# Layer norm of a streaming encoder layer: normalising on ScalarE, weight and bias as two plain VectorE operations

## What is computed

```python
def layer_norm(x, g, b):
    mu = xf.mean(-1); var = square(xf - mu).mean(-1)
    return ((xf - mu) * rsqrt(var + LN_EPS)) * g + b

def layer(x, ...):
    x = layer_norm(ALPHA * x + 0.5 * swiglu(x, ffn1_w_up, ffn1_w_down), ln1_g, ln1_b)
    h, new_buf, S_new = mixer(x, ...)      # one wide projection, short convolution, 4 retention heads, w_out
    x = layer_norm(ALPHA * x + h, ln2_g, ln2_b)
    x = layer_norm(ALPHA * x + 0.5 * swiglu(x, ffn2_w_up, ffn2_w_down), ln3_g, ln3_b)
```

## Time and profile before

| | before |
|---|---|
| median of 3 runs | 1916.72 us |
| lowest to highest | 1916.34 to 1918.64 us |
| the profiled execution | 1916.19 us, of which 1914.4 us are the span from first to last instruction |
| TensorE busy / VectorE busy / ScalarE busy / GpSimd busy | 1847.2 / 1109.4 / 463.7 / 650.9 us |
| mean granted TensorE clock | 0.987 of full |

### The profile page before, as it was taken

One profiled execution on the slowest core, in us unless ns is written; L12 is line 12 of the kernel. 1 busy time (PEld: TensorE's weight loads), 2 busy tenths in 40 slices (PEclk: granted clock), 3 DMA queues, 4 the chain that ended last, 5 costly groups with the idle time before them and its releaser, 6 DMA issues. The chain is left out here.

```text
span 1914.4 us, 26761 instructions
## 1 busy us (share of the span) xinstructions
PE 1847.2 (96%) x11200; PEld 1718.6 (90%) x11200; DVE 1109.4 (58%) x1395; ACT 463.7 (24%) x771; POOL 650.9 (34%) x428
## 2 busy tenths in 40 slices
PE   7899999998999999999999999999998899999996
PEld 6889899896889989989989999999987799899895
DVE  7667585577455355354354455334438677585666
ACT  4224243241061051051051000000004234242240
POOL 4323232232423423423423443444433233243230
PEclk9999999998999999999999999999998999999998
DMA  7333324403746646636647544444454323324312
GB/s 288 122 108 103 122 78 132 132 23 117 264 137 235 223 133 241 218 132 246 214 132 250 180 151 143 148 154 154 151 172 163 122 89 121 122 72 138 121 46 99
DMA packets 90328, 286.80 MB, mean 150 GB/s; under 512 B 8928, under 2 KB 11360, under 8 KB 89952
## 3 DMA queue, kind: packets, MB, share of 16 engines
q1 hardware_dynamic: 36288, 132.14, 22.4%
q0 software_dynamic: 24768, 90.19, 13.2%
q10 hardware_dynamic: 29152, 62.76, 8.9%
HBM read 260.86 MB, written 24.19 MB: 149 GB/s over the span
## 5 line engine op out<-in xcount | busy, mean ns | idle before, releaser
L391 POOL TENSOR_TENSOR wl<-raw,wh 128x1024 fp32r<-128x1024 f32 x172 | 434.1, 2524 | 92.5 <-DMA wh<-in_weights 89.8
L454 PE MATMUL ps<-xh,wl 128*128 128x320 f32 x1280 | 400.7, 313 | 22.6 <-POOL wl L391 14.0
L454 PE MATMUL ps<-xl,wh 128*128 128x320 f32 x1280 | 399.2, 312 | 0.0
L454 PE MATMUL ps<-xh,wh 128*128 128x320 f32 x1280 | 399.0, 312 | 0.0
L382 POOL DMA_DIRECT2D wh<-in_weights x172 | 97.2, 565 | 859.9 <-PE ps L454 797.5
L454 PEld LDWEIGHTS ps<-xh,wl 128*128 128x128 f32 x1280 | 243.8, 190 | 24.9 <-POOL wl L391 14.5
L454 PEld LDWEIGHTS ps<-xl,wh 128*128 128x128 f32 x1280 | 243.9, 191 | 0.3
L454 PEld LDWEIGHTS ps<-xh,wh 128*128 128x128 f32 x1280 | 243.6, 190 | 0.0
L454 PE MATMUL ps<-th,wql 128*128 128x320 f32 x640 | 197.7, 309 | 0.0
L454 PE MATMUL ps<-th,wqh 128*128 128x320 f32 x640 | 197.6, 309 | 0.0
L454 PE MATMUL ps<-tl,wqh 128*128 128x320 f32 x640 | 197.4, 308 | 0.0
(11 more groups left out here) (179 smaller groups left out, 3467.2 us busy)
## 6 DMA issues: line engine op xcount, KB each, us to landing
raw<-in_weights SPq DMA_DIRECT2D x172, 512.0 KB, 3.7
wh<-in_weights POOLq DMA_DIRECT2D x172, 512.0 KB, 4.8
qraw<-in_quads SPq DMA_DIRECT2D x80, 512.0 KB, 3.6
state<-in_state_ret ACTq DMA_DIRECT2D x48, 512.0 KB, 7.8
out_ret_sample<-state ACTq DMA_DIRECT2D x32, 512.0 KB, 5.3
xin<-in_x_T ACTq DMA_DIRECT2D x8, 320.0 KB, 6.8
z_scratch<-z ACTq DMA_DIRECT2D x1, 2560.0 KB, 8.8
z<-z_scratch ACTq DMA_DIRECT2D x1, 2560.0 KB, 10.0
```

Source lines behind the costliest of these rows:

```text
L391: pool.tensor_tensor(wl[:, r, :], raw[:, r, :], wh[:, r, :].bitcast(f32), ALU.subtract).then_inc(chunk_split, 1)
L454: ins = nc.tensor.matmul(out, lhs, rhs, start=start, stop=stop, skip_group_check=adds)
```

## The change

The subtraction of the mean and the multiplication by the inverse deviation move from VectorE's two fused operations to one ScalarE activation for each tile, z * inv + (-mean * inv), with scale and bias read for each partition. For that VectorE computes the bias, -mean * inv, with one small operation for each group of tiles, and raises a new semaphore, `deviation_ready`. ScalarE waits for it and normalises all tiles of the group in place, ahead of the copies of `to_T` (in stage 3 ahead of the second root, or of the stores). VectorE waits for each tile's activation, multiplies by the weight and adds the bias, with two `tensor_tensor` operations.

```diff
@@ ScalarE
+            def normalise(tiles):
+                dv.add()
+                act.wait_ge(deviation_ready, dv())
+                for t in tiles:
+                    result(nc.scalar.activation(z[:, t, :], z[:, t, :], ACT.Identity, bias=rt[:, 1, t:t + 1],
+                                                scale=rt[:, 2, t:t + 1]))
+
             def roots_and_to_T(keeps):
                 for tiles in (range(EARLY), range(EARLY, TT)):
                     roots(tiles[0], tiles[-1] + 1)
+                    normalise(tiles)
                     to_T(tiles, keeps)
@@ ScalarE, stage 3
-            roots(0, EARLY)
-            roots(EARLY, TT)
+            for tiles in (range(EARLY), range(EARLY, TT)):
+                roots(tiles[0], tiles[-1] + 1)
+                normalise(tiles)
             for t in range(TT):
                 act.wait_ge(z_ready, 2 * TT + t + 1)
@@ VectorE
-                inv_root(tiles[0], tiles[-1] + 1, LN_EPS / ALPHA ** 2)
+                c0, c1 = tiles[0], tiles[-1] + 1
+                inv_root(c0, c1, LN_EPS / ALPHA ** 2)
+                V.scalar_tensor_tensor(out=rt[:, 1, c0:c1], in0=mv[:, c0:c1, 0], scalar=-1.0, in1=rt[:, 2, c0:c1],
+                                       op0=ALU.mult, op1=ALU.mult).then_inc(deviation_ready, 1)

             def scale_and_shift(tiles):
                 for t in tiles:
-                    step(V.scalar_tensor_tensor(out=z[:, t, :], in0=z[:, t, :], scalar=mv[:, t, 0:1],
-                                                in1=lng[:, :], op0=ALU.subtract, op1=ALU.mult))
+                    act_result()
+                    step(tt(z[:, t, :], z[:, t, :], lng[:, :], ALU.mult))
                     after()
-                    V.scalar_tensor_tensor(out=z[:, t, :], in0=z[:, t, :], scalar=rt[:, 2, t:t + 1],
-                                           in1=lnb[:, :], op0=ALU.mult, op1=ALU.add).then_inc(z_ready, 1)
+                    tt(z[:, t, :], z[:, t, :], lnb[:, :], ALU.add).then_inc(z_ready, 1)
```

More of the change, by code:

```diff
@@ L257, in build_layer @@
         plain_summed = sem("plain_summed")
+        deviation_ready = sem("deviation_ready")
         x_kept = sem("x_kept")
@@ L835, in _ @@
         def _(act):
-            bk, root, ad, sn, hi = (Count() for _ in range(5))
+            bk, root, ad, sn, hi, dv = (Count() for _ in range(6))
             roles, merged = {}, {}
```

## The result

The changed kernel took 1922.76 us in the median of 8 runs (1921.9 to 1924.88), the kernel before 1917.63 us in 8 runs of the same kind (1915.91 to 1918.64). The ratio is 1.0029, with a 95% interval of 1.0019 to 1.0039: about 5.5 us slower. In a later comparison it was 1.0034 (1.0022 to 1.0047). The profiled execution took 1924.88 us, the longest of its eight; the one of before took 1916.19 us, near the shortest of its own. A difference of the two spans, 1923.1 and 1914.4 us, would overstate the change, so I compare stage ends, each from its own start.

What follows compares the result with a forecast made beforehand. VectorE's latency from the statistics to `z_ready` at the three stage ends, some 75 us, was taken as the bound, TensorE being busy elsewhere. 1.2 + 2.7 + 2.1 = +6.0 us gave 1922.5 us, range 1918.8 to 1926.0.

Steps and rivals of the forecast that it cites:

- The first activation: Head of each of six groups: VectorE waits 1.21 us for it, unhidden; with small operation and way, 1.42 us each group.
- The plain operations: Both VectorE passes over each tile: `tensor_tensor` instead of fused, 0.07 us less each, 0.14 us for a tile.
- Stage 3: End of the kernel: nothing hides the two groups' first activations; +2.1 us, bounds +1.7 and +2.8.
- Stage 1: End of stage 1: POOL's turn moves onto tile 1's addition, tile 2 ready 1.1 us later; +1.2 us, bounds -1.0 and +3.0.
- the wait for tile 4: Late group of stage 1: tile 4 ready 1.4 us after TensorE arrives, 0.95 us covered by transposes; 0.1 us counted.
- Stage 2: End of stage 2: POOL's turns delay tile 2, the late group gives some back; +2.7 us, bounds +0.8 and +4.4.
- The early part: Early group of stage 2: POOL holds tile 1's addition, then tile 2's multiplication; tile 2 ready 3.3 us later.
- -0.6 given back: Late group of stage 2: VectorE, coming later, meets less of POOL's work, so TensorE's wait for tile 4 shrinks; -0.6 us.
- The stretches outside the three ends: Rest of the kernel: shifts as a whole; a change of more than a microsecond there would prove the prediction wrong.
- (a): Stages 1 and 2: POOL's subtractions fall under `down` operations, saving long waits; +1.3 us, 1918.0; in full or one stage 0.16.
- (b): All six groups: Identity isn't in the root's table, so each pays a load of 1.28 us; 7.7 us, 1930; chance 0.04.
- (c): Stage 2: longer, more broken waits cool TensorE to a lower clock; +2 to +3 us more, 1925; chance 0.18.

Runs made afterwards that it cites:

- plain_only: Kernel before with the fused operations replaced by plain ones and nothing given to ScalarE (mean and deviation left out): 1916.8 us, ratio 0.9984 to 1.0001.
- s12: Kernel before with only the norms after stages 1 and 2 changed: 1920.7 us, ratio 1.0009 to 1.0026.
- yield_after: Changed kernel with three waits that hold back POOL's subtractions of chunks 27, 147 and 148 until given tiles are normalised: 1922.5 us, ratio to before 1.0027.
- s3: Kernel before with only the norm after stage 3 changed: 1919.6 us, ratio 1.0003 to 1.0021.
- first_fused: Changed kernel with tiles 0 and 3, the first of each group, normalised by VectorE's two fused operations: 1917.1 us, ratio to before 0.9998.
- mean_early: Changed kernel with ScalarE subtracting only the mean, before the root, and VectorE applying the inverse deviation in a fused operation: 1917.4 us, ratio to before 0.9999.
- quiet_before: Kernel before with POOL's subtraction of five weight chunks at the ends of stages 1 and 2 replaced by a memset: 1912.8 us, ratio 0.9963 to 0.9984.
- halves: Changed kernel with the activation and multiplication of each group's first tile split into two halves of 512 columns: 1922.9 us, ratio to before 1.0017 to 1.0038.

## Why the prediction was right, and where its terms were off

The forecast was 1922.5 us, slower; the median was 1922.8. By its steps:

**The first activation.** 1.21 us was put together from a copy and two per-partition reads the earlier trace rows; it takes 1.23 us. The Trainium skill's formula ("ScalarE: Activation LUTs", What ACT_TABLE_LOAD costs), 1.225 us, was the closer one. The shift of the first multiplication was 1.54 us in the early and 1.47 us in the late groups, not 1.42. In the early group VectorE starts 0.11 us after the activation's end (451.50 + 1.24 to 452.85), in the late one 0.03 us; why, I can't tell from the profile.

**The plain operations.** 1.22 us each and 0.12 us less for a tile, where 0.14 was forecast; plain_only has it alone.

**Stage 3: +2.1 forecast, +2.41 measured,** in every profile of the new form. The difference is the two sizes above. The stores did not become the bound: the last one is issued 0.04 us behind the last addition as before.

**Stage 1: +1.2 forecast, +1.72 measured.** The mechanism of the early group went as worked out, down to which operation POOL holds (tile 1's addition, 3.26 us) and that tile 2 is then free; tile 2 is ready 1.25 us later (forecast 1.1). The rest, 0.47 us, looks at first like the clock: the first half of the products, 48 of them, took 9.46 instead of 8.99 us, as 18 of them instead of 14 ran at the spacing of the 1.2 GHz level, and the chain behind the late tiles took 3.87 us as before. But s12 has the same timing on VectorE and did these products in 8.50 us, and its stage 1 still ended at 32.23 us, as TensorE then stood and waited for tile 4:

```profile
475.63 1.03 PE L675 MATMUL ps<-ident,z 128*128 128x128 f32 x8
477.64 1.09 PE L675 MATMUL ps<-ident,z 128*128 128x128 f32 x8 [0.97 <-DVE z L1173]
```

In the four profiles with tile 1's long addition and whole activations (changed, its repeat, s12, yield_after) the products take 8.50 to 9.47 us and the stage 32.2 to 32.3 us. VectorE's late group sets this end: it has tile 4 ready 29.4 us after the early aggregation, against 26.95 us before, where TensorE's arrival set the end. The term that was too small is thus the wait for tile 4. The prediction's own numbers give 1.4 - 0.95 = 0.45 us for it, and the sum took 0.1.

**Stage 2: +2.7 forecast, +3.12 measured.** The early part, +3.3, came as +3.2 (tile 2's end at 11.62 and 14.83 us after the aggregation's start). The -0.6 given back came too: from TensorE's arrival at the late tiles to the end of the stage it is 6.12 us before and 5.51 us now, as the wait for tile 4, 1.43 us, is gone and the chain of ScalarE's copies is the floor, as forecast. (It is 5.5 us in 11 of the 13 profiles.) What the prediction lacked is +0.46 us between tile 2's end and the first product: tile 2's transposes ran at the slower pace behind a slightly longer wait. Before and changed:

```profile
1444.47 1.09 PE L673 MATMUL ps<-ident,z 128*128 128x128 f32 x8 [3.06 <-DVE z L1339]
```

```profile
1450.28 1.97 PE L674 MATMUL ps<-ident,z 128*128 128x128 f32 x8 [3.19 <-DVE z L1169]
```

The products themselves took 9.65 and 9.71 us; 3.21 + 0.46 + 0.06 - 0.61 = 3.12. In s12 they took 8.70 us, and its stage 2 ended 1.0 us sooner than in changed: here the pace of the products does pass on to the end.

**The sum.** Here the forecast was better than its terms. They add to 7.25 us in the profiles, and the medians differ by 5.1 to 5.7. The step that failed is the one that took the single profile of before as typical. Its stage 2 ran in the course where POOL just misses tile 2's addition, by 0.13 us; s3, first_fused and mean_early, with the same early timing within 0.1 us, show the course of 32.3 to 32.9 us. Against these the change costs 1.2 to 1.9 us in stage 2, not 3.1. The profiled execution of before was also 1.4 us under the median of its kernel, a hint that I used only to centre the number. Too little in three terms and too short a starting point nearly cancelled, which is luck. So is the closeness of 1922.5 to 1922.8: the forecast change on the median of three runs, 5.8 us, is 0.7 above the measured 5.1, and that median, 1916.72, lies 0.9 under that of the eight. The stretches outside the three ends, which the prediction wanted within 1 us, changed by +1.07 us ahead of stage 1 (where the profiles scatter over 2.8 us, 446.64 to 449.47, with the same code), -0.18 and +0.54 us between the ends; they make up the rest of the 8.7 us between the two spans.

**The rivals.** (a) The order with POOL did not dissolve; it moved onto tile 1 as forecast. (b) The root's line has 11 table loads as before, and none stands before an Identity, so one table serves both. The Trainium skill ("ScalarE: Activation LUTs", Table sets: the hidden batching unit) has identity and copy in every set, and this trace agrees. (c) did not come: from the first product to the end of stage 2 the granted clock was 0.81 (1454.35 to 1469.57 us), against 0.82 in the like stretch before. The waits do cost clock, but in both kernels.

What stays open: how often each kernel takes which course in stage 2, as there is one profile for each, so that the sum of the stage ends is known to about 1 us only; why the pace of the first products differs by 1 us between profiles with the same timing; and why VectorE's start after an activation varies by 0.08 us.

## What to carry to other kernels

Handing a step to an idle engine helps only if a pass leaves the busy one. Here two passes stayed two, and the step stood at the head of a dependent chain, so its whole latency, 1.5 us with the way there and back, was added at the head of all six groups. In stage 3 both came through whole; in stages 1 and 2 other waits covered part. If a part of the step is known earlier (the mean, before the root), starting it there costs nothing. Before counting gains of tenths on VectorE, look for operations of unusual length beside POOL's, and let POOL wait where its result isn't wanted yet: that gave 3.3 us with three waits, where plain_only, with nothing handed to ScalarE at all, gained 0.6 us.

## What the runs showed of the hardware

- A VectorE operation with two SBUF inputs and a POOL `tensor_tensor` that reads SBUF exclude each other (3.24 instead of 1.28 us, 1.28 us in quiet_before). The one that has the turn keeps it to its end, and POOL, when it waits, gets its turn in the 0.04 us gap between two dependent VectorE operations. Which comes first could be read off the starts in the cases above but one (halves). It holds for tiny operations too: one of 128 x 2 took 2.33 us, and in the changed kernel even a `tensor_scalar` of 128 x 2 with one input took 0.68 us (at 1455.84) under POOL's 1455.21 to 1456.49. VectorE operations with one input in PSUM ran beside POOL at their usual 0.65 to 0.69 us, and so did statistics of `z`, which read SBUF once (two in 1.28 us from 1448.96 in s3, the second beside POOL's subtraction of 1449.43, as where POOL is idle). A memset on POOL held up nothing on `z`.
- An Identity with scale and bias for each partition over 128 x 1024 took 1.23 us, a copy with constants 1.047 us; followed by another it takes 1.14 us (3.51 us for three).
- TensorE's return from its waits costs beyond the wait: 9 to 22 of the first 48 products ran at the spacing of the lower clock level, up to 0.12 us lost for each. With VectorE's timing the same they took 9.46 us in changed and 8.50 us in s12, at granted clocks of 0.73 and 0.82.
